# The kv projection third instead of first, and the turned operand split straight from PSUM

## What is computed

```
xn     = rms_norm(x, norm_mix_g)
proj   = xn @ w_in                # 8448 columns: q_a 1024, k_a 128, v_a 128,
                                  # q_b, k_b, v_b 1024 each, gates 2 x 2048
o_a    = windowed attention with sinks (16 query heads, 2 key/value heads)
o_b    = chunked attention with relative bias (16 heads)
merged = sigmoid(g_a) * (o_a @ w_branch_a) + sigmoid(g_b) * (o_b @ w_branch_b)
h      = x + merged @ w_out
hn     = rms_norm(h, norm_ffn_g)
out    = h + (silu(hn @ w_gate) * (hn @ w_up)) @ w_down     # d_ff = 5632
```

## Time and profile before

| | |
|---|---|
| time, median of 3 runs | 1349.15 us (1349.11 to 1349.36) |
| span of the profiled execution | 1347.3 us |
| what lies around the span (the runs less the span) | 1.8 to 2.1 us |
| TensorE busy | 1331.1 us (99%) |
| VectorE busy | 743.3 us (55%) |
| ScalarE busy | 606.4 us (45%) |
| DMA, mean | 186 GB/s |

### The profile page before, as it was taken

How to read it: one execution, slowest core, us unless ns; L and a number is a source line. 1 busy time by engine, 2 the same in 40 slices (tenths; PEclk the granted TensorE clock), 3 DMA queues, 4 the chain that set the end, 5 groups by cost and what they waited for, 6 DMA issues and landing times.

```text
span 1347.3 us, 16021 instructions
## 1 busy us (share of the span) xinstructions
PE 1331.1 (99%) x6224; PEld 1100.3 (82%) x6224; DVE 743.3 (55%) x938; ACT 606.4 (45%) x781; POOL 33.5 (2%) x34
## 2 busy tenths in 40 slices
PE   7999999999999999999999999999999999999998
PEld 6888887777788888888888888888888888888887
DVE  6556556777455555565555555455545554555553
ACT  5454545555444444444444443344444434444442
POOL 1112110000000000000000000000000000000000
PEclk9999999999999999999999999999999999999999
DMA  8655655444565555555565555555555556555552
GB/s 260 198 202 165 210 188 182 147 148 143 206 200 188 188 187 188 188 185 187 188 193 185 191 188 201 194 188 188 189 186 188 187 200 196 195 187 187 187 187 94
DMA packets 129943, 251.23 MB, mean 186 GB/s; under 512 B 4624, under 2 KB 10832, under 8 KB 129632
## 3 DMA queue, kind: packets, MB, share of 16 engines
q1 hardware_dynamic: 129600, 250.37, 56.5%
q0 software_dynamic: 288, 0.10, 0.1%
HBM read 248.33 MB, written 2.12 MB: 186 GB/s over the span
## 4 chain that ended last, share of the span: by engine, by line
PE 95%; ACT 3%; DVE 1%; issue 0%; DMA 0%; DVEq 0%; SPq 0%; ACTq 0%
PE bank L948 30%; PE bank L950 30%; PE bank L949 30%; PE bank L877 2%; ACT prob L594 1%; PE bank L892 1%; ACT w_hi L494 1%; PE bank L917 1%; DVE staged L657 0%; PE bank L919 0%; PE bank L902 0%; DMA x_rows<-in_x 0%; PE bank L918 0%; DVE xT_lo L665 0%; DVE w_lo L648 0%
## 5 line engine op out<-in xcount | busy, mean ns | idle before, releaser
L648 DVE TENSOR_TENSOR w_lo<-raw,w_hi 128x1024 fp32r<-128x1024 f32 (+1 forms) x464 | 562.5, 1216 | 556.1 <-ACT w_hi L494 554.2
L494 ACT ACTIVATE w_hi<-raw 128x1024 fp32r<-128x1024 f32 (+1 forms) x464 | 487.6, 1052 | 694.8 <-PE bank L950 693.2
L948 PE MATMUL bank<-w_hi,xT_hi 128*128 128x512 f32 (+1 forms) x1248 | 488.6, 391 | 4.2 <-DVE w_lo L648 3.0
L950 PE MATMUL bank<-w_lo,xT_hi 128*128 128x512 f32 (+1 forms) x1248 | 483.2, 387 | 0.0
L949 PE MATMUL bank<-w_hi,xT_lo 128*128 128x512 f32 (+1 forms) x1248 | 482.9, 387 | 0.0
L948 PEld LDWEIGHTS bank<-w_hi,xT_hi 128*128 128x128 f32 x1248 | 234.9, 188 | 53.7 <-issue 2.6
L950 PEld LDWEIGHTS bank<-w_lo,xT_hi 128*128 128x128 f32 x1248 | 234.9, 188 | 47.9
L949 PEld LDWEIGHTS bank<-w_hi,xT_lo 128*128 128x128 f32 x1248 | 235.1, 188 | 45.8
L948 PE MATMUL bank<-w_hi,oT_hi 128*128 128x512 f32 x480 | 187.0, 390 | 0.0
L950 PE MATMUL bank<-w_lo,oT_hi 128*128 128x512 f32 x480 | 186.8, 389 | 0.0
L949 PE MATMUL bank<-w_hi,oT_lo 128*128 128x512 f32 x480 | 186.7, 389 | 0.0
(11 more groups left out here) (109 smaller groups left out, 496.2 us busy)
## 6 DMA issues: line engine op xcount, KB each, us to landing
raw<-in_w_in SPq DMA_DIRECT2D x64, 1024.0 KB, 5.3
raw<-in_w_ffn_gate SPq DMA_DIRECT2D x44, 1024.0 KB, 5.2
raw<-in_w_ffn_up SPq DMA_DIRECT2D x44, 1024.0 KB, 5.1
raw<-in_w_ffn_down SPq DMA_DIRECT2D x44, 1024.0 KB, 5.0
raw<-in_w_out SPq DMA_DIRECT2D x16, 1024.0 KB, 5.0
raw<-in_w_branch_a SPq DMA_DIRECT2D x8, 1024.0 KB, 5.0
raw<-in_w_branch_b SPq DMA_DIRECT2D x8, 1024.0 KB, 4.9
x_rows<-in_x SPq DMA_DIRECT2D x4, 512.0 KB, 7.7
```

The costliest lines, as they stand in the source:

```text
L494: A(w_hi[:, p % SPLIT_SLOTS, 0:w], raw[:, c % RAW_SLOTS, (p % 2) * w:(p % 2 + 1) * w], ACT.Copy).then_inc(hi_ready, 1)
L648: V.tensor_tensor(w_lo[:, p % SPLIT_SLOTS, 0:w], raw[:, p // 2 % RAW_SLOTS, (p % 2) * w:(p % 2 + 1) * w], w_hi[:, p % SPLIT_SLOTS, 0:w].bi ...
L948: M(sums, x_hi, w_hi[:, p % SPLIT_SLOTS, w], start=kt == 0, stop=False)
L950: ins = M(sums, x_hi, w_lo[:, p % SPLIT_SLOTS, w], start=False, stop=kt == j.kts - 1)
```

## The change

The kv job stands third, behind the two jobs for q_a; the first job is a qk job with 512 columns, so its chunks are 1 MB and the first half chunk 512 KB. x stays on SyncE's queue, each group ahead of the chunk with its number. The turned weights of the norm come ahead of x's group 0. A group of x or h is turned with two k-tiles to a bank (both halves of the tokens side by side), and each pair of k-tiles is split straight from PSUM: ScalarE writes `xT_hi` with the norm's weight as scale (two instructions of 256 columns a pair), VectorE computes PSUM times weight less `xT_hi` in one instruction for each k-tile; `staged` isn't used. The first job's splits of weights stand ahead of the operand's; groups 2 and 3 are turned after pieces 1 and 3. Each piece of the first job waits for its own pair. The squares of x move to pieces 0 and 1 of the second job. For h all of it stands at k = 5.

```diff
-    job("kv", 0, "w_in", 0, qa, 2 * kva, kt, "x", 0)
     for n in range(qa // COLS):
         job("qk", n, "w_in", 0, n * COLS, COLS, kt, "x", 0)
+    job("kv", 0, "w_in", 0, qa, 2 * kva, kt, "x", 0)
...
+            def gained_to_hi(first_bank, kt0, g0, pair0):
+
+                for i in range(GROUP // 2):
+                    act.wait_ge(x_turned, pair0 + i + 1)
+                    for c in range(2):
+                        kt = 2 * i + c
+                        ins = A(xT_hi[:, kt0 + kt, :], bank[first_bank + i][:, c * S:(c + 1) * S], ACT.Copy,
+                                scale=g_col[:, g0 + kt:g0 + kt + 1])
+                    ins.then_inc(gained_hi, 1)
...
-                if j.kind == "out" and k == 6:
-                    scaled_to_hi(NB + j.n, j.n)
+                if j.kind == "out" and k == 5:
+                    gained_to_hi(T_BANK, j.n * GROUP, KT + j.n * GROUP, KT // 2 + 2 * j.n)
...
                 for k in range(j.pieces):
+                    split_hi(j, k)
                     if j.prev is None and k % 2 == 0:
-                        scaled_to_hi(k // 2, k // 2)
-                    split_hi(j, k)
-                    if j.prev is None and k in (5, 7):
+                        if k == 0:
+                            act.wait_ge(g_ready, 1)
+                        g = k // 2
+                        gained_to_hi(4 + 2 * (g % 2), g * GROUP, g * GROUP, 2 * g)
+                    if j.prev is jobs[0] and k < T:
                         for q in range(NB):
                             act.wait_ge(x_landed[q], 16)
...
+            def gained_to_lo(first_bank, kt0, g0, pair0):
+
+                for i in range(GROUP // 2):
+                    dve.wait_ge(gained_hi, pair0 + i + 1)
+                    for c in range(2):
+                        kt = 2 * i + c
+                        ins = V.scalar_tensor_tensor(xT_lo[:, kt0 + kt, :], bank[first_bank + i][:, c * S:(c + 1) * S],
+                                                     g_col[:, g0 + kt:g0 + kt + 1],
+                                                     xT_hi[:, kt0 + kt, :].bitcast(F32), ALU.mult, ALU.subtract)
+                    ins.then_inc(xT_ready, 1)
...
             def turn_x(g):
                 pe.wait_ge(x_landed[g], 16)
-                if g >= 2:
-                    pe.wait_ge(scaled_ready, g - 1)
-                for t in range(T):
-                    for c in range(GROUP):
-                        ins = turn(bank[4 + 2 * (g % 2) + t][:, c * P:(c + 1) * P],
-                                   x_rows[:, t, g * COLS + c * P:g * COLS + (c + 1) * P], ident[:])
-                ins.then_inc(x_turned, 1)
+                for i in range(GROUP // 2):
+                    if g >= 2:
+                        pe.wait_ge(xT_ready, 2 * (g - 2) + i + 1)
+                    for c in range(2):
+                        for t in range(T):
+                            col = g * COLS + (2 * i + c) * P
+                            ins = turn(bank[4 + 2 * (g % 2) + i][:, c * S + t * P:c * S + (t + 1) * P],
+                                       x_rows[:, t, col:col + P], ident[:])
+                    ins.then_inc(x_turned, 1)
...
                 pe.wait_ge(lo_ready, p + 1 + j.off)
+                if j.prev is None:
+                    pe.wait_ge(xT_ready, k + 1)
...
             pe.wait_ge(ident_ready, 1)
-            turn_x(0)
             pe.wait_ge(mix_landed, 16)
             turn(bank[0][:, 0:KT], mix_rows[:], ident[0:KT, 0:KT]).then_inc(g_turned, 1)
+            turn_x(0)
             turn_x(1)
...
-                    if j.prev is None and k in (0, 2):
-                        turn_x(k // 2 + 2)
+                    if j.prev is None and k in (1, 3):
+                        turn_x((k - 1) // 2 + 2)
```

More of the change, by code:

```diff
@@ L135, in plan @@
             j.set = sets
-            sets += 1
+            sets += j.kind != "out"
     at = 0
@@ L283, in build @@
         x_turned = sem("x_turned")
-        scaled_ready = sem("scaled_ready")
-        scaled_hi = sem("scaled_hi")
+        gained_hi = sem("gained_hi")
         xT_ready = sem("xT_ready")
@@ L340, in set_read @@
             return {"qk": lambda: (qk_ready, T * (j.set + 1)), "kv": lambda: (qk_ready, T * (j.set + 1)),
-                    "bb": lambda: (mT_ready, T * (j.n + 1)), "out": lambda: (scaled_ready, NB + j.n + 1),
+                    "bb": lambda: (mT_ready, T * (j.n + 1)), "out": lambda: (xT_ready, KT // 2 + 2 * (j.n + 1)),
                     "up": lambda: (fT_ready, T * (j.n + 1))}[j.kind]()
@@ L553, in follow @@
                 if j.kind == "ga" and k == 3:
-                    act.wait_ge(x_turned, NB)
+                    act.wait_ge(x_turned, KT // 2)
                     out_of_psum(j, lambda t: gate_a[:, t, columns(j)], slice(0, COLS)).then_inc(ga_ready, 1)
@@ L611, in do_job @@
                 for k in range(j.pieces):
+                    split_hi(j, k)
                     if j.prev is None and k % 2 == 0:
-                        scaled_to_hi(k // 2, k // 2)
-                    split_hi(j, k)
-                    if j.prev is None and k in (5, 7):
+                        if k == 0:
[3 more added lines that the diff above has]
+                    if j.prev is jobs[0] and k < T:
                         for q in range(NB):
                             act.wait_ge(x_landed[q], 16)
-                        t = (k - 5) // 2
-                        A(squares[:, t, :], x_rows[:, t, :], ACT.Square,
-                          accum_out=x_ss[:, t:t + 1]).then_inc(x_ss_ready, 1)
+                        A(squares[:, k, :], x_rows[:, k, :], ACT.Square,
+                          accum_out=x_ss[:, k:k + 1]).then_inc(x_ss_ready, 1)
                     if j.prev is not None:
@@ L650, in split_lo @@
                                 w_hi[:, p % SPLIT_SLOTS, 0:w].bitcast(F32), ALU.subtract).then_inc(lo_ready, 1)
-            def scale_rows(first_bank, g0, n):
-                if n:
-                    dve.wait_ge(xT_ready, n)
-                for t in range(T):
[L657 to L668, removed]
+            def gained_to_lo(first_bank, kt0, g0, pair0):
[7 more added lines that the diff above has]
+                    ins.then_inc(xT_ready, 1)
             def turned_to_lo(dst_hi, dst_lo, at_group, sets_before, ready):
@@ L733, in follow @@
                     if k == 5:
-                        dve.wait_ge(turned, j.set + 1)
-                        scale_rows(T_BANK, KT + j.n * GROUP, NB + j.n)
+                        gained_to_lo(T_BANK, j.n * GROUP, KT + j.n * GROUP, KT // 2 + 2 * j.n)
                         if j.n == NB - 1:
@@ L738, in follow @@
                             V.tensor_reduce(h_sum[:], h_ss[:], AX.X, ALU.add).then_inc(h_sum_ready, 1)
-                    if k == 6:
-                        scaled_to_lo(NB + j.n, j.n)
                 if j.kind == "gate" and k == 3:
@@ L820, in do_job @@
                 for k in range(j.pieces):
+                    split_lo(j, k)
                     if j.prev is None and k % 2 == 0:
                         g = k // 2
[L823 to L826, removed]
+                        gained_to_lo(4 + 2 * (g % 2), g * GROUP, g * GROUP, 2 * g)
                     if j.prev is None and k == 6:
@@ L862, in turn_x @@
                 pe.wait_ge(x_landed[g], 16)
-                if g >= 2:
-                    pe.wait_ge(scaled_ready, g - 1)
-                for t in range(T):
-                    for c in range(GROUP):
-                        ins = turn(bank[4 + 2 * (g % 2) + t][:, c * P:(c + 1) * P],
-                                   x_rows[:, t, g * COLS + c * P:g * COLS + (c + 1) * P], ident[:])
-                ins.then_inc(x_turned, 1)
+                for i in range(GROUP // 2):
[7 more added lines that the diff above has]
+                    ins.then_inc(x_turned, 1)
             def turn_set(j):
                 pe.wait_ge(*staged_for(j))
-                src = h[:, :, columns(j)] if j.kind == "out" else staged
+                if j.kind == "out":
+                    for i in range(GROUP // 2):
+                        for c in range(2):
+                            for t in range(T):
+                                col = j.n * COLS + (2 * i + c) * P
+                                ins = turn(bank[T_BANK + i][:, c * S + t * P:c * S + (t + 1) * P],
+                                           h[:, t, col:col + P], ident[:])
+                        ins.then_inc(x_turned, 1)
+                    return
+                src = staged
                 for t in range(T):
@@ L924, in operand_ready @@
                 g = kt // GROUP
-                if j.prev is None:
-                    pe.wait_ge(xT_ready, g + 1)
                 if j.kind == "ba" and j.first and g == 0:
@@ L931, in operand_ready @@
                 if j.kind == "gate" and j.first:
-                    pe.wait_ge(xT_ready, NB + g + 1)
+                    pe.wait_ge(xT_ready, KT // 2 + 2 * (g + 1))
                 if j.kind == "down" and j.first:
```

## The result

The changed kernel takes **1350.88 us** (median of 15 runs, 1349.88 to 1353.36) against 1349.13 for the kernel before; the ratio is 1.0016, 95% interval 1.0009 to 1.0024. It is 1.75 us slower: clear of its interval, and within the 0.2% that I had called "no change". The forecast was 1350.0 us. The profiled execution is one of the eleven, at 1350.38 us, with a span of 1348.3.

What follows compares the result with a forecast made beforehand. The prediction took TensorE, busy 99% of the span, as the bound. From 1349.15 us, less 1.8 at the start, plus 2.7 for the wait in kv, it got 1350.05, forecast as 1350.0 us, range 1348.1 to 1352.3.

Steps and rivals of the forecast that it cites:

- Bound: Whole kernel: TensorE busy 99% of the span; the change can win only in the first 30 us or lose by waits.
- The last group of h: Feed-forward part: ready at 626.4 us before, about 3 us earlier after; margin of 4.6 us only grows, cost 0.
- First matmul: Start: the first qk job's first matmul at 12.6 us, bounds 12.1 and 13.5, where it was before.
- step (1): Start: x's group 1 lands at 10.65 us by the queue's mean 318 GB/s; bounds 10.1 and 11.5.
- Clock at the start: Start: clock rises at 15.3 us as before; 2.7 us at half rate lose 1.35 us, bounds 0 and 2.7.
- Start in sum: Start: 16.9 us lost instead of 18.7, gain 1.8 us; bounds from a gain of 3.8 to a loss of 1.3.
- The stop in kv: Third job: heads need 9.9 us, pieces cover 7.2, so TensorE waits 2.7 us; bounds 2.4 and 3.5.
- Around the span: Profiled execution outside its span: the same 1.8 us as before.
- The time: Whole kernel: 1350.0 us, no change that can be told; span 1348.2 us.
- Rival A: Stop in kv: clock falls to 1.2 GHz in or behind it, costing 1.4 to 3.1 us; 1351.4 to 1353.1; chance 0.14.
- Rival B: Start: group 1 at 10.1 us, clock up earlier, gain 3.0 to 3.8 less 2.7; 1348.1 to 1348.9 us; chance 0.22.

Runs made afterwards that it cites:

- the eleven: The changed kernel's runs from 1349.88 to 1351.69 us; its other four runs took 1353.03 to 1353.36 us.
- the order alone: The kernel before with the kv job third and the old split of x: 1350.71 us, ratio 1.0016.
- the kernel kept busy: Changed kernel with kv first again, new split, TensorE turning the identity into an unused bank while waiting for x: 1343.91 us, ratio 0.9961 against the kernel before.
- the three kernels with this stop: Changed kernel, 1350.88 us; kernel before with kv third and old split, 1350.71; changed kernel with x's group 1 ahead of the first chunk's second half, 1348.26.

## Why the prediction was right, and where its sizes were off

- **Bound.** Right but for the 0.2 us of the attention part: outside the first 80 us nothing else changed; TensorE has no wait around the out jobs. The last group of h was ready at 622.54 + 1.65 = 624.2 instead of 626.4, in a trace that runs 1 us later by then.
- **First matmul.** I said 12.6 us (12.1 to 13.5) and it was 13.2 in the timeline, with a long distance behind it, and 13.55 in the chain, 0.95 late. The mis-sized term is step (1): group 1 at 10.65 by the mean rate of 318 GB/s, measured 11.6, my high bound. The bound that came from the transfer that had the same bytes before it was the right one; the mean rate over the whole start was not. From 9.0 to 11.5 us, just before the group lands, the DMA moves 261 GB/s, where the kernel before (first line) has 321; what slows it is not known.

```profile
9.00:11.50 2.50, 1.97 (x8) 1.57 (x8) 1.38 (x2) 1.90 (x3) 0.00 (x0) 1.00 0.95 321
```

```profile
9.00:11.50 2.50, 0.00 (x0) 0.00 (x0) 2.50 (x5) 2.19 (x5) 0.00 (x0) 1.00 0.93 261
```

- **Clock at the start.** I took 1.35 us with the rise at 15.3. In the profiled execution it rose at 15.2 and cost 0.85, since the matmuls began later; in the three other profiled kernels whose group 1 comes as late it rose at 16.4, 17.2 and 17.3. Two microseconds of rise are 1 us of time; that would account for the spread of the ordinary runs and for a median 0.5 above the profiled run, though the traces of those runs are not at hand.
- **Start in sum.** 17.4 us lost, forecast 16.9: the late group cost 0.95 more and the clock 0.5 less, which is luck. The gain is 1.6 instead of 1.8, since the kernel before lost 19.0 and not 18.7. The second job began at 39.2, forecast 38.7; the fourth at 76.4, forecast near 76.5.
- **The stop in kv.** 2.3 us, forecast 2.7, and just under my low bound of 2.4. GpSimd's L462, which was L463 before, took 0.57 us in this place instead of 1.10; its median in the changed kernel is 1.11, so this is no gain of the change. Nothing more was late behind it, as said. Its removal gave 2.35 us.
- **Around the span.** I took 1.8 us. It is 2.1 for all kernels with the new split (2.1 to 2.2) and 1.8 for the three with the old one: 0.3 us that I had not counted. The cause stays open.
- **The time.** 1350.0 forecast, 1350.9 measured. In the profiled execution the span grew by 1.0 us, of which the terms above give -1.6 + 2.3 + 0.2 = +0.9; forecast was -1.8 + 2.7 = +0.9. That these agree so closely is partly luck, for the stop came 0.4 short while the start and the attention part cost 0.4 more. What is left is the 0.3 around the span and the 0.5 by which the median lies above the profiled run.
- **Rival A** is real and I gave it 0.14 as if it were the case of all runs; it is the case of some, 4 of 15, which lie 2.3 us above the rest (1353.1 and 1350.8). The Trainium skill ("TensorE: Matmul & The Clock Gate", the HAM clock gate) had the mechanism right in both directions: in the trace of the order alone an idle stretch gave the clock back, with a granted clock of 0.76 over 7 us, and activity released it early in the kernel kept busy, where group 1's turns took 1.09 us. The same section of the Trainium skill warns only of longer stops than this one of 2.3 us; here the measurement decides.
- **Rival B** named the way to win (group 1 early) but not that the change itself moved it the other way.
- What I did not see at all: that kv first with the new split is 3.5 us faster than before. I weighed the split only inside the new order, where pieces of 2.72 us hide the old one too.

## What to carry to other kernels

When a change has an order and a cheaper step in it, cost each without the other: here each hides the same start, so together they gain once, and the order's own prices (a transfer behind twice the bytes, a follow-up chain of 9.5 us under a job with 7.2 us of cover) eat the gain. Put the short job where its predecessor leaves nothing to finish. And price a stop of the matrix engine not only by its length: look for runs in which the clock falls behind it.

## What the runs showed of the hardware

A stop of 2.3 us between busy stretches sometimes cost TensorE's upper clock and sometimes not. One trace shows the fall (granted clock 0.50 behind the stop): eight turns took 1.97 us instead of 1.09 and some seven matmuls behind them ran slow, 1.5 us in all. That it fell in the 12 of 37 runs of the three kernels with this stop that lie 2.1 to 2.4 us high is inferred, from their mean granted clock of 0.998 and from the runs without the stop, of which none is high. With turns of a constant into an unused bank in the stop no run was high (0 of 11), and such turns at the start raised the clock early (1.7 us). The DMA queue needed 2.6 us more for 0.5 MB ahead of a group of x, about 200 GB/s, though it moved 330 GB/s on average between 5 and 15 us.
